# A gathered expert sum, taken row by row instead of in pairs of rows

## What is computed

```
s1, i1 = lax.top_k(s[:, :, 0], PEER_TOPK)
s2, i2 = lax.top_k(s[:, :, 1], PEER_TOPK)
...
act = jax.nn.gelu(jnp.einsum('thkd,td->thk', u_tab[idx], xb)) * wts
return jnp.einsum('thk,thkd->td', act, v_tab[idx])
```

## Time and profile before

| what | value |
|---|---|
| device time, median of 3 runs | 3575.82 us (3573.34 to 3580.6) |
| span of the profiled execution | 3751.8 us |
| time of the profiled execution outside its span | not given |
| granted TensorE clock, mean | 0.819 of full |
| TensorE matmul busy | 2608.3 us |
| VectorE busy | 1998.1 us |
| GpSimd busy | 1507.8 us |
| ScalarE busy | 710.4 us |
| moved by DMA | 1156.38 MB, of it 849.51 MB by GpSimd's queue |

### The profile page before, as it was taken

How to read it: one execution, slowest core, us unless ns; L and a number is a source line. 1 busy time by engine, 2 the same in 40 slices (tenths; PEclk the granted TensorE clock), 3 DMA queues, 4 the chain that set the end, 5 groups by cost and what they waited for, 6 DMA issues and landing times.

```text
span 3751.8 us, 35602 instructions
## 1 busy us (share of the span) xinstructions
PE 2608.3 (70%) x12888; PEld 1195.8 (32%) x12888; DVE 1998.1 (53%) x5016; ACT 710.4 (19%) x1775; POOL 1507.8 (40%) x1609
## 2 busy tenths in 40 slices
PE   6687766655556675655679666556654798899998
PEld 1233222111112221111144221112311385676765
DVE  0465656656657656776422476667698436221411
ACT  1121111211112311211132112112221213020300
POOL 0025555555665666566600056666466400000000
PEclk8888888788776887676679778777877899999999
DMA  8779998999998999899923489999999776667677
GB/s 316 269 275 342 342 344 326 367 402 401 365 361 320 356 363 340 320 364 361 359 100 122 149 326 384 361 364 332 348 354 334 298 260 255 219 251 249 215 255 258
DMA packets 363676, 1156.38 MB, mean 308 GB/s; under 512 B 33712, under 2 KB 33968, under 8 KB 362476
## 3 DMA queue, kind: packets, MB, share of 16 engines
q0 software_dynamic: 232144, 849.51, 60.5%
q1 hardware_dynamic: 130940, 304.36, 22.7%
q10 hardware_dynamic: 416, 0.23, 0.0%
HBM read 1152.84 MB, written 1.15 MB: 308 GB/s over the span
## 4 chain that ended last, share of the span: by engine, by line
PE 42%; DVE 19%; DMA 14%; issue 7%; POOL 7%; another core or an unknown queue 5%; ACT 5%; SPq 0%; DVEq 0%; ACTq 0%; POOLq 0%
PE PS L1155 10%; PE PS L1089 8%; POOL BIG L2357 7%; DVE BIG L1965 7%; PE PS L1360 6%; PE PS L1378 6%; DMA BIG<-in_p_v_dram,IDX 6%; DMA BIG<-in_p_u_dram,IDX 5%; PE PS L1254 2%; PE PS L1348 1%; PE PS L1117 1%; DVE SC L2151 1%; DMA WR<-in_w_mod_dram 1%; ACT dg L1552 1%
## 5 line engine op out<-in xcount | busy, mean ns | idle before, releaser
L1155 PE MATMUL PS<-BIG,dg 64*64 64x512 f32 x6144 | 1059.3, 823 | 849.7 <-ACT dg L1552 383.5
L2357 POOL DMA_INDIRECT BIG<-in_p_u_dram,IDX x768 | 734.5, 956 | 1163.2 <-ACT PS L1539 417.8
L1965 DVE CUSTOM_DVE_ANT_0 BIG<-BIG,PS 128x1024 f32<-128x1024 f32 x768 | 927.8, 1215 | 325.8 <-DMA BIG<-in_p_u_dram,IDX 294.3
L2357 POOL DMA_INDIRECT BIG<-in_p_v_dram,IDX x768 | 732.0, 953 | 313.7 <-issue 180.6
L1155 PEld LDWEIGHTS PS<-BIG,dg 64*64 64x64 f32 x6144 | 274.9, 172 | 1520.9 <-issue 963.4
L1089 PE MATMUL PS<-WR,HT 128*128 128x512 f32 x640 | 294.4, 614 | 9.9 <-DMA WR<-in_a_w_in_dram 6.6
L1552 ACT ACTIVATE dg<-twin,ACTV 128x64 f32<-128x64 f32 x768 | 208.0, 336 | 345.2 <-PE PS L1155 149.8
L1360 PE MATMUL PS<-HT,WR 128*128 128x128 f32 x2048 | 256.1, 285 | 5.9 <-DMA WR<-in_mlp_w_dram 5.9
L1360 PEld LDWEIGHTS PS<-HT,WR 128*128 128x128 f32 x2048 | 247.3, 200 | 15.8 <-issue 8.9
L1378 PE MATMUL PS<-WR,BIG 128*128 128x512 f32 x512 | 226.0, 596 | 0.0
L1089 PEld LDWEIGHTS PS<-WR,HT 128*128 128x128 f32 x640 | 122.3, 196 | 177.0 <-issue 167.9
(11 more groups left out here) (320 smaller groups left out, 2709.7 us busy)
## 6 DMA issues: line engine op xcount, KB each, us to landing
WR<-in_mlp_w_dram SPq DMA_DIRECT2D x128, 1024.0 KB
WR<-in_w_mod_dram SPq DMA_DIRECT2D x48, 1024.0 KB
WR<-in_b_w_in_dram SPq DMA_DIRECT2D x18, 1024.0 KB
WR<-in_a_w_in_dram SPq DMA_DIRECT2D x16, 1024.0 KB
WR<-in_p_w_q_dram SPq DMA_DIRECT2D x16, 1024.0 KB
BIG<-in_dsa_w_dram POOLq DMA_DIRECT2D x16, 1024.0 KB, 7.6
BIG<-in_p_u_dram,IDX POOLq DMA_INDIRECT x768
BIG<-in_p_v_dram,IDX POOLq DMA_INDIRECT x768
```

The costliest lines, as they stand in the source:

```text
L1155: mm = self.e.matmul(pv[64 * i:64 * i + 64, 2 * r + n, :], dg[p, :], row[p, n * 512:n * 512 + 512], start=h == 0 and j == 0, stop=h == 7 a ...
L1965: self.e.tensor_tensor_reduce(row, row, xp, 1.0, 0.0, ALU.mult, ALU.add, m.ACTV[:, u % 4, j:j + 1]).then_inc(*self.done("dot", l, u, j))
L2357: self.e.indirect_dma_start(row, None, m.A[f"p_{table}"], bass.IndirectOffsetOnAxis(ap=m.IDX[:, u % 4, j:j + 1], axis=0)).then_inc(*m.GR.l ...
```

## The change

`v_sum` is called at every beat, for one pick. TensorE waits for that pick's diagonal and landing, emits four products (both halves of columns, both halves of partitions) into the half of the output that belongs to the pick's parity, signals, and frees that row's slot and diagonal alone. ScalarE writes one diagonal at each beat instead of two at each odd one. The accumulation flags are given so that the first pick of either parity starts its half and the last of either parity ends it. The products, the diagonals and the gathers are the same in number.

```diff
                 if u:
                     self.v_gather(l, u - 1, j)
-                    if j % 2:
-                        self.v_sum(l, u - 1, j - 1, b, h)
+                    self.v_sum(l, u - 1, j, b, h)
                 next(nxt, None)
...
     def v_sum(self, l, u, j, b, h):
 
-        m = self.m
-        pv = m.PV.of(l, b)
-        self.wait_ge(m.act.at("diagonal", l, u, j + 1), m.GR.landed("v", l, u, j), m.GR.landed("v", l, u, j + 1))
+        m, i = self.m, j % 2
+        pv, row, dg = m.PV.of(l, b), m.GR.of("v", l, u, j), m.DG.of(l, u, j)
+        self.wait_ge(m.act.at("diagonal", l, u, j), m.GR.landed("v", l, u, j))
         for n in range(2):
-            for i in range(2):
-                row, dg = m.GR.of("v", l, u, j + i), m.DG.of(l, u, j + i)
-                for r in range(2):
-                    p = slice(64 * r, 64 * r + 64)
-                    mm = self.e.matmul(pv[64 * i:64 * i + 64, 2 * r + n, :], dg[p, :],
-                                       row[p, n * 512:n * 512 + 512], start=h == 0 and j == 0,
-                                       stop=h == 7 and j == 14)
+            for r in range(2):
+                p = slice(64 * r, 64 * r + 64)
+                mm = self.e.matmul(pv[64 * i:64 * i + 64, 2 * r + n, :], dg[p, :], row[p, n * 512:n * 512 + 512],
+                                   start=h == 0 and j < 2, stop=h == 7 and j > 13)
         mm.then_inc(*self.done("sum", l, u, j))
-        if h == 7 and j == 14:
+        if h == 7 and j == 15:
             self.done.note("block sum", l, b)
-        for i in range(2):
-            m.GR.free(("v", l, u, j + i), self.done.last())
-            m.DG.free((l, u, j + i), self.done.last())
+        m.GR.free(("v", l, u, j), self.done.last())
+        m.DG.free((l, u, j), self.done.last())
...
     def v_sum(self, l, u, j, b, h):
         m = self.m
-        for i in (j, j + 1):
-            dg = m.DG.take(l, u, i)
-            self.wait_ge(m.dve.at("active", l, u), m.dve.at("twin"), *m.DG.emptied(l, u, i))
-            self.e.activation(dg[:, :], m.twin[:, :], ACT.Copy, scale=m.ACTV[:, u % 4, i:i + 1]).then_inc(
-                *self.done("diagonal", l, u, i))
+        dg = m.DG.take(l, u, j)
+        self.wait_ge(m.dve.at("active", l, u), m.dve.at("twin"), *m.DG.emptied(l, u, j))
+        self.e.activation(dg[:, :], m.twin[:, :], ACT.Copy, scale=m.ACTV[:, u % 4, j:j + 1]).then_inc(
+            *self.done("diagonal", l, u, j))
```

## The result

The change made the kernel slower: 3621.2 us in the median of 4 runs (3614.1 to 3626.8) beside 3578.2 us before, a ratio of 1.0138 (95% interval 1.0117 to 1.0160). A second series gave 1.0156 (1.0130 to 1.0183). I had forecast 3533 us and a range of 3440 to 3640; the time lies in the range and on the other side of no change.

The account below looks back on a forecast made before the run. No engine was taken as the bound throughout; the slot ring limits at times, and DMA is 0.95 busy in quiet stretches. Terms -60 - 45 + 50 + 10 = -45 us, scaled by 0.953 to -43, gave 3533 us, range 3440 to 3640.

Parts of the forecast that it names:

- quiet stretches: 900:1200, 1500:1860 and 2150:2500 us, where little but the expert loop runs; freeing the even row earlier was to give -60 us.
- Part 1: The even row's slot, freed earlier, shortens GpSimd's waits for the sum: -60 us in quiet and -45 us in busy stretches.
- busy stretches: 260:600, 600:900, 1200:1500 and 2500:2990 us, where TensorE has other work; earlier freeing was to give -45 us.
- Part 2: TensorE's products: rows separated by other work use half the array, 169 us extra, 30% on the path: +50 us.
- Part 3: TensorE's wait for the even row holds up the next expert's routing product and scores: +10 us.
- Part 4: TensorE's clock may rise as its work spreads evenly; bounds 0 and about -105 us, taken as 0.
- rival (c): TensorE is never long idle in the loop and stays at the upper clock level: 3433 us; chance 0.14.
- Rival (a): TensorE becomes the bound where other work splits rows: +165, -105 and +10 make +70, 3643 us; chance 0.26.

Follow-up runs that it names:

- the new profile: The kernel before, unedited, profiled again on a chip of the faster kind; span 3568.1 us, ratio 1.0018 against other runs of itself.
- freeing by pair: The changed kernel, but the even row's slot and diagonal are handed back by the odd row's signal; 3627.7 us, 1.0171 of the kernel before.
- the series with four parts: The changed kernel, but the four products of each row go to four different parts of the array; 3567.9 us, 0.9995 of the kernel before.
- the combined version: Against the kernel before: four array parts per row, both rows at the odd beat with own signals, one diagonal each beat; 0.9836 slower chip, 0.9864 faster.

## Why the prediction was wrong, point by point

**What bounds the kernel.** Half right. The read of the quiet stretches was the failure. The earlier trace rows had 0.95 of DMA time and 351 to 358 GB/s, by the span from a chip of the slower kind. On the faster kind the quiet units of those stretches (903:1027, 1530:1690 and 2251:2375 of the new profile) run at 409 GB/s and 1.03, and each takes 41 us before and after. The rows also held a warning that I passed over: a span 5% longer than the median of the runs was no detail to be scaled away with a factor of 0.953, since the new profile has another balance of the resources, not the same one stretched.

**Part 1, -105 us.** This is the step that failed, and the term that turned the sign; without it the sum would have been +60. The quiet stretches' -60 were 0 on this chip, and of the busy stretches' -45 at most some 7 were there: freeing by pair adds 6.6 us, hardly clear of nothing. The prediction took the waits for the sum as time that GpSimd wins back when the even row is freed early: two thirds of its bound in the quiet stretches, a fifth in the busy ones. GpSimd does wait 95 us less for the sum, but 78 us more for the dot products, and freeing by pair turns most of that round again (+148, -118). GpSimd then waits for another slot of the full ring, so the wait was mostly backpressure, the mark of consumers that are not yet done. I had written that the rows lie in their slots, and then priced a fifth of the waits all the same, from one restart.

**Part 2, +50 us.** The mechanism was right. The size came near by luck, as said below. Separately signalled rows on different parts do overlap: x16 records in 1.96 us where two rows stand side by side, with no fraction more. Changed kernel:

```profile
391.76 1.96 PE L1152 MATMUL PS<-BIG,dg 64*64 64x512 f32 x16
393.66 3.70 PE L1088 MATMUL PS<-WR,HT 128*128 128x512 f32 x8
397.29 1.93 PE L1152 MATMUL PS<-BIG,dg 64*64 64x512 f32 x8
399.15 3.70 PE L1088 MATMUL PS<-WR,HT 128*128 128x512 f32 x8
```

A lone row costs 1.93 us on two of the four parts and 1.09 us on all four. The Trainium skill has it that tiles operate independently ("TensorEngine Tiling (Array Packing)", Key Properties); the trace agrees, in 1.96 us for two rows and 1.93 us for one. The lone rows cost 1.6% by the series with four parts (1.0156 against 0.9995), some 57 us. The busy time grew by 341 us and not by 169, because rows are alone in the quiet stretches as well, where it is harmless. So 17% of it reached the path, not 30%: twice the time and half the share, and the two errors cancel.

**Part 3, +10 us.** Right in kind: the routing product stands behind row 0, ScalarE's wait for it doubles and VectorE's grows by 50 us. Measured by moving the sums to the end of the beat it is 13 us, net of a later freeing; the bounds of 18 to 97 were for a cost that nothing makes up. On the slower chip the same run gave 1.0176 beside 1.0169 for freeing by pair, with no run of the change to hold it against, so the 13 us stand for the faster kind alone.

**Part 4, 0.** The clock rose, from 0.846 to 0.923 in the mean, as rival (c) had it: in the quiet stretch TensorE idled about 1.5 and 3.1 us in turn between pairs before and 0.6 us between rows after, and it kept the upper level of 2.4 GHz with half the array in use. What the Trainium skill says of idle gaps between bursts ("TensorE: Matmul & The Clock Gate", HAM oscillation), that they bring the clock back down, agrees with both traces. The higher clock was worth nothing where the DMA engines set the pace. What it gave back in the busy stretches (0.83 to 0.88 in units 18 to 25) was not isolated; it did not outweigh the lone rows there.

**The sum.** With the measured sizes: 0 to -7 for freeing, +13 for the place, and lone rows for the rest. Those effects are not independent, and by the runs they add to 1.4 to 1.6%, 43 to 55 us. Rival (a) named this, with its place and the price of a row; it had +165 for lone rows where some 50 were measured, -105 for freeing where 0 to -7 was, and so came to +70 with two terms wrong in opposite ways.

## What to carry to other kernels

Before a batched product is split into single calls, ask whether each call still fills the parts of the array that the batch filled, or whether its neighbours in the queue do. Here it cost 1.4 to 1.6% where they did not, and nothing (0.9995) where the parts were laid out over the columns of the single row. A producer's wait is not yet a price: the wait put down to one releaser can pass to the next. Here 148 us of it came and 118 us went, and the time moved by 7; compare all of the engine's idle time before its gathers, and ask whether the transfers have room. And a profile whose span is 5% off the runs' median may have another balance than the runs; profile the kernel before on the chip that is timed, or widen the range.

## What the runs showed of the hardware that was not expected

- The same kernel takes 3566 to 3568 us on three chips and 3761 us on a fourth, each within 1% over its series. Quiet units move 409 GB/s on the faster kind and 363 on the slower (1638:1777 of the combined version there). One chip in one series is all there is of the slower kind, and why it is slower is open. The verdicts kept their sign: the change freed by pair is 1.0171 and 1.0169, with the sum at the end of the beat 1.0117 and 1.0176, the combined version 0.9864 and 0.9836.
- The granted clock stood at 1.00 in a quiet stretch (1560:1710 of the change) in which each row used two of the four parts of the array.
- TensorE at 71% busy over the span was a bound all the same: with 487 us more of its time in the trace, the kernel took 185 us more.
